# Attention of the first layer on the whole 128x128 array: zero-padded queries, paired values, and raw weight buffers of half the size

## The reference, cut to what matters

```python
def stick_breaking(q, k, v):          # q, k, v: 1 x 512 tokens x 16 heads x 64
    # for each block of 128 queries, kend = the keys up to the block's end
    logits = einsum('bqhd,bkhd->bhqk', q_block, k[:, :kend]) * scale
    mask = ki < qi
    log_fail = where(mask, log_sigmoid(-logits), 0)
    between = cumsum(log_fail, axis=3, reverse=True) - log_fail
    w = where(mask, exp(log_sigmoid(logits) + between), 0)
    out = einsum('bhqk,bkhd->bqhd', w, v[:, :kend])
```

## Time and profile before

| what | before |
|---|---|
| median of 3 runs | 1540.63 us (1539.97 to 1542.06) |
| span of the profiled execution | 1539.1 us |
| PE busy, share of the span | 1475.6 us, 96% |
| PE weight loads | 1130.7 us, 73% |
| DVE busy | 717.5 us, 47% |
| ACT busy | 539.9 us, 35% |
| POOL busy | 182.2 us, 12% |
| chain that ended last | PE 85%, DVE 7%, ACT 3%, POOL 2%, issue 2% |
| mean granted TensorE clock | 0.983 of full speed |

### The profile page before, as it was taken

How to read it: one execution, slowest core, us unless ns; L and a number is a source line. 1 busy time by engine, 2 the same in 40 slices (tenths; PEclk the granted TensorE clock), 3 DMA queues, 4 the chain that set the end, 5 groups by cost and what they waited for, 6 DMA issues and landing times.

```text
span 1539.1 us, 17384 instructions
## 1 busy us (share of the span) xinstructions
PE 1475.6 (96%) x6957; PEld 1130.7 (73%) x6957; DVE 717.5 (47%) x1069; ACT 539.9 (35%) x910; POOL 182.2 (12%) x143
## 2 busy tenths in 40 slices
PE   6899999999999999999899999998997999999999
PEld 4777778766666678877787666566786888888887
DVE  4764444534444445342635566364745343433343
ACT  4553333544334333233424354343323231222221
POOL 0117420013333300000000022121000000000000
PEclk9999999999999999999999999898999999999999
DMA  5122123220010043222431100000231323232222
GB/s 189 63 74 83 55 69 110 83 82 28 28 55 28 28 192 137 90 83 82 136 111 51 55 28 28 1 28 1 98 107 55 110 83 109 83 109 98 94 89 76
DMA packets 20432, 119.63 MB, mean 78 GB/s; under 512 B 2304, under 2 KB 3584, under 8 KB 8192
## 3 DMA queue, kind: packets, MB, share of 16 engines
q1 hardware_dynamic: 19776, 117.47, 21.7%
q10 hardware_dynamic: 576, 1.05, 0.3%
HBM read 113.27 MB, written 4.19 MB: 76 GB/s over the span
## 4 chain that ended last, share of the span: by engine, by line
PE 85%; DVE 7%; ACT 3%; POOL 2%; issue 2%; DMA 0%; SPq 0%; DVEq 0%; ACTq 0%
PE bank L718 82%; POOL arena L1957 2%; PE bank L882 2%; PE bank L1053 1%; PE bank L776 1%; DVE arena L1439 1%; DVE arena L1852 1%; DMA arena<-in_x 0%; DVE wlo L1421 0%; DVE a_lo L1613 0%; ACT whi L1118 0%; ACT arena L1240 0%; DVE arena L1588 0%; ACT L1203 0%; ACT a_hi L1226 0%
## 5 line engine op out<-in xcount | busy, mean ns | idle before, releaser
L718 PE MATMUL bank<-a_hi,whi 128*128 128x512 f32 x848 | 342.1, 403 | 0.7 <-DVE a_lo L1613 0.7
L718 PE MATMUL bank<-a_hi,wlo 128*128 128x512 f32 x848 | 332.1, 392 | 0.0
L718 PE MATMUL bank<-a_lo,whi 128*128 128x512 f32 x848 | 332.0, 392 | 0.0
L718 PE MATMUL bank<-arena 128*64 128x128 f32 (+9 forms) x1496 | 287.0, 328 | 14.3 <-DVE arena L1748 8.9
L1421 DVE TENSOR_TENSOR wlo<-wraw,whi 128x2048 fp32r<-128x2048 f32 (+1 forms) x97 | 223.4, 2303 | 90.5 <-ACT whi L1118 89.9
L1118 ACT ACTIVATE whi<-wraw 128x2048 fp32r<-128x2048 f32 (+1 forms) x97 | 183.6, 1893 | 181.1 <-PE bank L718 180.9
L718 PEld LDWEIGHTS bank<-arena 128*64 128x64 f32 (+2 forms) x1496 | 183.1, 171 | 75.3 <-issue 47.4
L718 PEld LDWEIGHTS bank<-a_hi,whi 128*128 128x128 f32 x848 | 160.3, 189 | 38.3 <-issue 7.1
L718 PEld LDWEIGHTS bank<-a_hi,wlo 128*128 128x128 f32 x848 | 160.0, 189 | 34.3
L718 PEld LDWEIGHTS bank<-a_lo,whi 128*128 128x128 f32 x848 | 160.4, 189 | 31.7 <-issue 1.0
L718 PE MATMUL bank<-whi,a_hi 128*128 128x512 f32 x320 | 128.2, 401 | 5.8 <-DVE a_lo L1903 3.0
(11 more groups left out here) (224 smaller groups left out, 1608.2 us busy)
## 6 DMA issues: line engine op xcount, KB each, us to landing
wraw<-in_wblk SPq DMA_DIRECT2D x93, 1024.0 KB, 4.9
wraw<-in_wblk SPq DMA_DIRECT2D x4, 768.0 KB, 4.4
arena<-in_x SPq DMA_DIRECT2D x4, 512.0 KB, 6.0
arena<-in_x SPq DMA_DIRECT2D x1, 2048.0 KB, 7.8
spill<-arena SPq DMA_DIRECT2D x4, 512.0 KB, 8.9
arena<-spill SPq DMA_DIRECT2D x1, 2048.0 KB, 7.9
out<-arena SPq DMA_DIRECT2D x8, 256.0 KB, 2.0
arena<-in_w1k SPq DMA_DIRECT2D x1, 1024.0 KB, 15.8
```

Of the source, the lines that this page charges most:

```text
L718: return nc.tensor.matmul(o, lhsT, rhs, start=start, stop=stop, **kw)
```

## The change

It has four parts.

1. **Queries padded.** A buffer `qz` (128 x 2 x 512) holds the queries of two heads. POOL fills it: `pad_query(h)` multiplies all 128 partitions of the pair's queries by a column that is 1 for the head's own 64 partitions and 0 for the others. The logits' matmul then contracts over 128 partitions; the other head's keys are multiplied by zeros.
2. **Values of both heads.** The stationary side of the sum over values is 128 columns, both heads of the pair. The bank gets 128 rows, and DVE copies the 64 that belong to the head, as before.
3. **Raw buffers halved.** `wraw` is two buffers of 128x1024. SP, ACT and DVE treat each block in two pieces. SP loads a piece when the same piece of the block before has been used; ACT rounds the pieces of block n+1 at slices 0 and 2 of block n, DVE takes them at slices 2 and 4 (it took the block at slice 3).
4. **Waits.** PE waits for the second piece of a block at slice 2 (blocks of the form "feature") or 1 ("token").

```diff
@@ SP @@
-                if n >= 2:
-                    sp.wait_ge(s_lo, n - 1)
-                cols = width(n)
-                sp.dma_start(wraw[n % 2][:, 0:cols], dram["wblk"][n][:, 0:cols]).then_inc(s_w[n % 2], 16)
+                for i in range(2):
+                    if n >= 1:
+                        sp.wait_ge(s_lo, 2 * n + i - 1)
+                    cols = piece(n, i)
+                    sp.dma_start(wraw[i][:, 0:cols.stop - cols.start], dram["wblk"][n][:, cols]).then_inc(s_w[i], 16)
@@ PE, gemm @@
-                    pe.wait_ge(s_hi, n + 1)
-                    pe.wait_ge(s_lo, n + 1)
+                    pe.wait_ge(s_hi, 2 * n + 1)
+                    pe.wait_ge(s_lo, 2 * n + 1)
+                if s == (2 if b["form"] == "feature" else 1):
+                    pe.wait_ge(s_hi, 2 * n + 2)
+                    pe.wait_ge(s_lo, 2 * n + 2)
@@ PE, stick @@
+                    if qt == 0:
+                        pe.wait_ge(s_qz, h + 1)
-                    mm(ps[:, 0:kend], qf[rows, h // 2, P * qt:P * qt + P], kf[rows, h // 2, 0:kend], True, False)
+                    mm(ps[:, 0:kend], qz[:, h % 2, P * qt:P * qt + P], kf[:, h // 2, 0:kend], True, False)
...
-                        last = mm(bank[BANK_O][rows, P * (v % 4):P * (v % 4) + P], vt[:, kb, h * HD:h * HD + HD],
+                        last = mm(bank[BANK_O][:, P * (v % 4):P * (v % 4) + P], vt[:, kb, pair],
@@ ACT, gemm @@
-                    if s[2] == 0:
-                        round_weights(s[1] + 1)
+                    if s[2] in (0, 2):
+                        round_weights(s[1] + 1, s[2] // 2)
@@ DVE, gemm @@
-                    if s[2] == 3:
-                        rest_of_weights(s[1] + 1)
+                    if s[2] in (2, 4):
+                        rest_of_weights(s[1] + 1, s[2] // 2 - 1)
@@ POOL @@
+            def pad_query(h):
+                if h >= 2:
+                    pool.wait_ge(s_qk, NT * (h - 1))
+                g_.tensor_scalar(qz[:, h % 2, :], qf[:, h // 2, :], V("half", h % 2), None, ALU.mult).then_inc(s_qz, 1)
...
+                    if u == 0:
+                        pool.wait_ge(*end_sem("q"))
+                        pad_query(0)
+                    if u % NT == 0 and u // NT + 1 < SH:
+                        pad_query(u // NT + 1)
```

More of the change, by code:

```diff
@@ L65 @@
 BLK = 2048
+PIECE = 1024
 def weave(*streams, weights=None):
@@ L386 @@
 VEC = Columns([("b_gate", 16), ("conv_w", 48), ("conv_b", 12), ("dt_bias", 16), ("a_log", 16), ("d_skip", 16),
-               ("q_norm", 1), ("k_norm", 3), ("lower", 8)])
+               ("q_norm", 1), ("k_norm", 3), ("lower", 8), ("half", 2)])
 CST2 = Columns([("w2", 2 * HD), ("pos", CL), ("heads", 4), ("one", 64)])
@@ L423, in sem @@
             return ctx.enter_context(nc.semaphore(name))
-        wraw = [sb(f"wraw{i}", [P, BLK]) for i in range(2)]
+        wraw = [sb(f"wraw{i}", [P, PIECE]) for i in range(2)]
         whi = [sb(f"whi{i}", [P, BLK], F32R) for i in range(2)]
@@ L437, in emit @@
         zerob = sb("zerob", [P, 2], BF16)
+        qz = sb("qz", [P, 2, T])
         stat = sb("stat", [P, STAT])
@@ L592, in emit @@
         s_tr, s_wT, s_pv, s_o = sem("s_sb_turned"), sem("s_sb_wT"), sem("s_sb_summed"), sem("s_sb_out")
+        s_qz = sem("s_query_padded")
         s_t, s_tround, s_mg = sem("s_product"), sem("s_product_rounded"), sem("s_merged")
@@ L620, in width, with piece @@
             return BLOCKS[n]["kn"] * sum(c for _, c in BLOCKS[n]["spans"])
+        def piece(n, i):
+            return slice(PIECE * i, min(PIECE * i + PIECE, width(n)))
         def used_by_pe(n):
@@ L1037, in stick @@
                     h, qt = divmod(u, NT)
-                    rows, kend = slice(HD * (h % 2), HD * (h % 2) + HD), P * (qt + 1)
+                    kend = P * (qt + 1)
                     if u >= 2:
                         pe.wait_ge(s_sig, u - 1)
+                    if qt == 0:
+                        pe.wait_ge(s_qz, h + 1)
                     ps = bank[BANK_LOGITS + u % 2]
@@ L1057, in stick @@
                     h, qt = divmod(v, NT)
-                    rows = slice(HD * (h % 2), HD * (h % 2) + HD)
+                    pair = slice(P * (h // 2), P * (h // 2) + P)
                     pe.wait_ge(s_wT, v + 1)
@@ L1109, in link, with round_weights @@
                 act.wait_ge(s_ac, chain[0])
-            def round_weights(n):
+            def round_weights(n, i):
                 if n >= NB:
                     return
-                act.wait_ge(s_w[n % 2], 16 * (n // 2 + 1))
-                if n >= 2:
+                act.wait_ge(s_w[i], 16 * (n + 1))
+                if n >= 2 and i == 0:
                     act.wait_ge(*used_by_pe(n - 2))
-                cols = width(n)
-                A(whi[n % 2][:, 0:cols], wraw[n % 2][:, 0:cols], ACT.Copy).then_inc(s_hi, 1)
+                cols = piece(n, i)
+                A(whi[n % 2][:, cols], wraw[i][:, 0:cols.stop - cols.start], ACT.Copy).then_inc(s_hi, 1)
             def round_small(kind):
@@ L1320, in _ @@
                     if s[1] == "dt":
-                        round_weights(0)
+                        for i in range(2):
+                            round_weights(0, i)
                     act.wait_ge(s_tile, DONE[s[2]])
@@ L1414, in mark, with rest_of_weights @@
                 return chain[0]
-            def rest_of_weights(n):
+            def rest_of_weights(n, i):
                 if n >= NB:
                     return
-                dve.wait_ge(s_hi, n + 1)
-                cols = width(n)
-                v.tensor_tensor(wlo[n % 2][:, 0:cols], wraw[n % 2][:, 0:cols], f32(whi[n % 2][:, 0:cols]),
+                dve.wait_ge(s_hi, 2 * n + i + 1)
+                cols = piece(n, i)
+                v.tensor_tensor(wlo[n % 2][:, cols], wraw[i][:, 0:cols.stop - cols.start], f32(whi[n % 2][:, cols]),
                                 ALU.subtract).then_inc(s_lo, 1)
@@ L1880, in _ @@
                 if s[0] == "small":
-                    rest_of_weights(0) if s[1] == "dt" else lower_bound()
+                    if s[1] == "dt":
+                        for i in range(2):
+                            rest_of_weights(0, i)
+                    else:
+                        lower_bound()
                 if s[0] == "dt":
@@ L1981, in lay_out @@
                         d_skip=rows(d_skip[0]),
-                        q_norm=np.tile(q_norm_2[0].reshape(HD, 1), (2, 1)), k_norm=np.tile(k_norm_2[0].T, (2, 1)),
+                        q_norm=np.tile(q_norm_2[0].reshape(HD, 1), (2, 1)), k_norm=np.tile(k_norm_2[0].T, (2, 1)), half=np.arange(P)[:, None] // HD == np.arange(2)[None, :],
                         lower=np.concatenate([cols(hgrn_lb_logits_2[0]), cols(hgrn_lb_logits_2[1])], axis=1)).items():
```

## The result

The changed kernel takes 1503.95 us (median of 4 runs, 1502.37 to 1504.61) against 1540.3 us before (4 runs beside them, 1536.17 to 1542.06): ratio 0.9767, 95% interval 0.9751 to 0.9782. The forecast was 1505.5 us, 1493 to 1520. The profiled execution took 1503.91 us and spans 1502.1 us, 37.0 less than the one of before.

The account below looks back on a forecast made before the run. PE was taken to bound the attention stage, busy 221.6 of 225 us. 1539.1 - 36.5 - 2.5 + 6 - 2 = 1504.1 us in the profile, 1505.5 us for the median; range 1493 to 1520.

Parts of the forecast that it names:

- PE's sequence: Attention stage: full-array logits and values, cheaper transposes save 0.52 to 0.62 us a unit, 0.57 taken; 36.5 us over 64 units.
- the pair on 64 rows loses more than its exit, so I go by the rows: Attention logits: gains taken from profile rows, 0.19 us in the pair, instead of four shape changes at 0.10 each, 25.6 us.
- the rival to which I gave 0.06: Attention stage on PE: only changes of tile shape cost, so 25.6 us go instead of 36.5, about 1513 us; chance 0.06.
- The rival of bare loads: Logits and value passes: with all tiles on the whole array each load stands before its matmul, 1592 us; chance 0.03.
- PE's wait for POOL: Attention transposes: DVE's weight block, taken in halves, no longer delays POOL's 512-column product; 2.5 us of PE waits go.
- The new wait: Values of n=2: faster PE waits for DVE's copy behind the n=4 scan, 0.38 us a head, 6 us (3 to 8).
- the first rival: Attention stage: other engines set the pace, paddings stalled to 3.8 us or copy waits of 0.8 us, 1513 to 1521; chance 0.13.
- POOL's padding: Attention stage: 16 operations of 128x512 at 1.3 us each on POOL, hidden ahead of the product for n=1.
- Halved buffers in other stages: Norm and transpose stages: halves of weight operations may fall into gaps of the chain; 2 us gained (-6 to +3).
- Transfers: Weight loads: a half block lands no slower than a block's 4.9 us, within 8.3 us before ACT needs it; hidden.

Follow-up runs that it names:

- copy_first: Changed kernel with DVE's copy of a unit's result ahead of the scan of the same unit instead of behind it: 1495.79 us.
- logits_more_64: Kernel with only the halved raw buffers (old shapes, 64 rows), every logits matmul of the first layer's attention done twice into the same place: 1567.31 us.
- rest_at_slice_3: Changed kernel with both of DVE's pieces of the weights' lower parts taken at slice 3 of a block, instead of at slices 2 and 4: 1508.33 us.
- pieces_only: Changed kernel with both shapes and POOL's padding taken back, so only the raw weight buffers are halved: 1535.1 us.
- pad_twice: Changed kernel with POOL padding each head's queries twice, the second behind the first: 1504.11 us.
- pair_no_pad: Changed kernel with only the padding taken back: logits on 64 rows as before, values on 128 columns: 1525.43 us.
- pad_no_pair: Changed kernel with only the paired values taken back: logits on 128 rows, values on 64 columns as before: 1515.18 us.

## Why the prediction was right, point by point

- **PE's sequence, forecast 36.5 us, measured 40.** From the last weights matmul ahead of a unit to the second behind it, the time less two plain slices went from 2.01 to 1.37 us (n=4), from 1.69 to 1.06 (n=1, in `copy_first`, without the wait), from 2.22 to 1.61 (n=2) and from 2.34 to 1.71 (n=3). That is 0.63 a unit instead of 0.57, just over the range of 0.52 to 0.62: two full-array value passes and the weights matmul behind them take 0.45, which leaves nothing for an exit, where I had allowed for 0.09 at one end of the range. The gain of the unit with n=4 was carried over to the others as if only their columns differed; they differ in value passes too, two to eight, and it held because the price is one of the visit.
- **The cause given for it was wrong.** The step that failed is "the pair on 64 rows loses more than its exit, so I go by the rows". The rows were right and the reading was not. One visit to 64 rows costs 0.10 in front, some 0.10 between its first and second pass and some 0.09 behind; one to 64 columns costs some 0.32 in all, 0.09 of it ahead. The sum was the same either way, since every visit to 64 rows here has just two passes. For the cause, the right number was luck. For a kernel with more passes in a visit it would have been far off: for `logits_more_64` I expected 47.8 us and the rival's 34 came. The Trainium skill, "TensorEngine Tiling (Array Packing)", Key Properties, says that a change of the tiling mode drains TensorE. The traces agree that a change costs time, once for each visit; whether what it costs is a drain, no row shows. My own price for it was too low: 25.6 us for four changes at 0.10, where 0.63 a unit is 0.16 a change. So the rival to which I gave 0.06 had the cause right and its price wrong.
- **The rival of bare loads fell.** All tiles are on the whole array now, and value passes start 0.11 us apart (two more of them make 0.22 us: 0.91 and 1.13 for six and eight), as 64-column ones did before. The Trainium skill, "TensorE: Matmul & The Clock Gate", What overlaps and what doesn't, says that a load overlaps matmuls in flight only when the row group differs. The trace shows otherwise. In the timeline of the changed kernel's loads, the one below begins with the matmul of 441.11, on the same full array, and takes 0.19 us, while the weights matmuls go on starting every 0.23 us:

```profile
441.12 0.19 PEld L725 LDWEIGHTS bank<-b_hi,wlo 128*128 128x128 f32 x1
```

- **PE's wait for POOL, forecast -2.5 us: right in its reason**: put back to one place the pieces bring it back (`rest_at_slice_3`). From start to start it was worth more, 3.8 us in the stage (`pieces_only`).
- **The new wait, forecast 6 us (3 to 8), measured 10, outside these bounds.** Place, count and cause were right: once a head, at the values that follow the n=4 scan. The size was not: 0.64 us a head lies between my 0.38 and the 0.8 of the first rival. From the mask at 440.38 to the copy's end at 443.30 are 2.92 us (forecast 2.93), and PE would have come at 440.38 + 2.51, with 442.55 + 0.34 for the transposes, so 0.41 early (forecast 0.35). What was mis-sized is above all the release, 0.15 us from the copy's end to the first pass in place of 0.03, and 0.08 more for passes that start from standstill, which I had at nothing. 0.64 x 16 = 10.2. The view of waits shows 7.2 of it; the distance of starts shows all.
- **POOL's padding, forecast hidden: right** at 1.67 us instead of 1.3 (`pad_twice`).
- **Halved buffers in other stages, forecast -2 (-6 to +3): not borne out.** `pieces_only` comes to 0 there (-1.6 ahead of the attention, +1.5 behind it), but 1.6 us of that is a short stretch at the lower clock near 690 that it lacks. The changed kernel stands at -1.3 ahead, +2.9 between the stage's end and 941, and the 7.6 us gained after that come with the clock (last section). DVE's piece takes 1.30 us in the mean where I had 1.19, so two are 0.28 more than the whole and not 0.05. Pieces of weights now stand seven times in the chain that ended last, 7.9 us in all, in place of six times and 12.3 us, so the gain that I looked for in the chain is there and is spent again; first and last of them, view of the chain:

```profile
50.51 1.23 DVE wlo L1434
...
1116.08 0.95 ACT whi L1130
```

- **Transfers, forecast hidden: right for PE.** A piece lands in 3.7 us, and no wait of PE for the weights has come. ACT now waits for a piece at times, 10.8 us in all (the line of L1130 above), which it never did for a whole block.

That the sum held so closely is in part luck: 3.5 us too little at PE's sequence and 1.3 at the wait for POOL were set off by 4 too little at the new wait, and what the clock gave stood in for the gain that the halved buffers did not bring.

## What to carry to other kernels

Where small matmuls on a part of the array stand between full ones, count visits and not passes: a visit to 64 rows cost 0.29 us and one to 64 columns some 0.32 us here, so padding to the full shape pays where visits are short and an idle engine can do the padding. When the bounding engine gets faster, look for the next thing it waits on and whether the producer has that work queued behind something longer: moving one 0.29 us copy ahead of a 1.23 us scan shortened the stage by 9.5 us, nearly all of the 10.2 that the new wait had cost. Price such a wait from start to start, with the release and the refill, and not from the view of waits.

## What the runs showed of the hardware that was not expected

**The same stage takes 198 to 210 us, with the granted clock.** Between 941 and 1064 us of the old scale nothing on PE was changed. Windows over the same piece of program (859 to 1064 on that scale) in four kernels, columns as in the earlier trace rows, the clock behind the engines: before,

```profile
858.90:1063.90 205.00, 195.19 (x1006) 132.10 (x1005) 113.09 (x281) 81.64 (x197) 36.33 (x30) 0.93 0.06 21
```

`pair_no_pad`,

```profile
839.80:1049.40 209.60, 198.50 (x1006) 134.17 (x1005) 113.34 (x285) 82.88 (x201) 36.30 (x30) 0.92 0.07 21
```

`pad_no_pair`,

```profile
838.40:1036.10 197.70, 186.62 (x1007) 126.43 (x1006) 113.19 (x285) 82.72 (x200) 36.30 (x30) 0.98 0.07 22
```

and the changed kernel:

```profile
826.30:1024.70 198.40, 186.90 (x1003) 127.29 (x1006) 113.26 (x285) 82.80 (x201) 36.30 (x30) 0.98 0.07 22
```

DVE and POOL do the same work to 0.3 us; PE's busy time and the length go with the granted clock, 0.92 for the longest and 0.98 for the shortest. In the stretches at the lower level (1.2 GHz, half of the full 2.4) the kernel before spends 2 x 13.7 us there, `pair_no_pad` 2 x 13.7 and 6.8, `pad_no_pair` 6.8 and the changed kernel 2 x 3.4. The kernel before shows it by itself too: its 15 runs beside the second group lie either at 1536.0 to 1536.7 us with a clock of 0.987, or at 1540.6 to 1542.2 with 0.983. So some 5 us, 0.3%, come and go with the clock between runs of one kernel, and up to 12 between kernels (209.6 against 197.7). As an estimate, a stretch at half clock costs at most half of its length: 34.1 us in `pair_no_pad` against 6.8 in `pad_no_pair` are up to 13.7 us, so the clock is enough for the 10 us between the two halves of the change. It is in the changed kernel's 36 too: 7.6 us are gained in this stage and 2.7 lost behind it, where 17.1 us at the lower level stand against 6.8 before. That the longer ones have the lower clock is what the windows show; why a kernel gets the one or the other was not settled. Differences of up to some 10 us between kernels here should be read from the stage itself in the trace and not from the medians.

**POOL's multiply by a column** (128x512, float32) takes 1.67 us, more than its product of two tiles of that size, 1.28 us, though it reads one tile less.
